# An RWKV scan with transposes shared by two chunks and two heads, and a Fourier stage over even and odd halves

## The chip, the cores and the metric

One core of one Trainium2 chip runs the whole program: a two-layer diffusion block, then a second block with an RWKV-7 mixer, an HGRN2 mixer and a mixture of experts, all in float32. The metric is the device time of one execution in microseconds. TensorE is PE in the profile (PEld its weight loads), VectorE is DVE, ScalarE is ACT, GpSimd is POOL and SyncE is SP.

## The reference, cut to what matters

Two pieces of it are touched. The Fourier mixing is a real part of a 2-D transform over tokens and the 128 channels of a group; there are four groups, once for 512 latent tokens and once for 256 context tokens:

```python
def fourier_mix(u):
    B_, L, _ = u.shape
    ug = u.reshape(B_, L, FOURIER_GROUPS, FOURIER_GROUP_DIM).astype(jnp.float32)
    f = jnp.fft.fft2(ug, axes=(1, 3), norm='ortho').real
    return f.reshape(B_, L, FOURIER_WIDTH).astype(u.dtype)
```

The RWKV scan is a recurrence over 768 tokens in either direction, for 8 heads of 64 channels:

```python
def _rwkv7_scan(r, w, k, v, a, b, s0, reverse, emit):
    def step(s, inp):
        r_t, w_t, k_t, v_t, a_t, b_t = inp
        sa = jnp.einsum('bhvk,bhk->bhv', s, a_t)
        s = s * w_t[:, :, None, :] + sa[..., None] * b_t[:, :, None, :] + v_t[..., None] * k_t[:, :, None, :]
        y = jnp.einsum('bhvk,bhk->bhv', s, r_t) if emit else None
        return s, y
```

## The kernel before, in words

The program is a row of stages, each a block with one hand-written instruction list per engine, semaphores between them and a barrier at the end. All data lies in one SBUF tensor (`arena`) and one PSUM tensor of 8 banks of 512 columns (`psum`).

**The even input stage** (`even_in`) makes, among others, u, the input of the Fourier mixing, as four tiles of 128 channels by 768 tokens. ACT copies each from PSUM. DVE has nothing to do with u; in that part of its list it copies the turned values vt.

**The Fourier stage** (`fourier`, profile lines L1421 to L1460). `channels(g)` multiplies six token tiles of group g by a 128x256 table of cosines and sines (L1421), ACT copies the result (L1453), and `tokens(g)` multiplies by token tables: for the latent tokens 4 tiles, cosine (L1431) and sine (L1432), 512 columns each, into one bank, for the context tokens 2 tiles and 256 columns (L1434, L1435). DVE copies the 768 columns of both banks (L1460), and the next group's `tokens` waits for that copy, as it writes the same banks. SP loads the tables at the end of `even_in`.

**The RWKV scan** (`rwkv_scan`). The recurrence is cut into 12 chunks of 64 tokens in each direction, 24 items, which alternate between the directions. The 8 heads stand as 4 pairs: partitions 0 to 63 hold one head of a pair (`h` = 0), 64 to 127 the other. Every product is thus 8 matmuls of 64x64, two at a time on different quarters of the array. `side_by_side(a, b)` interleaves two such products, a on the two straight quarters and b on the two crossed ones (results for the other half of the partitions). A helper makes each product's matmuls, so that the profile shows the helper's line: `same` L2301, `turned` L2304, `adding` L2316, `wide_keys` L2321, `wide_rp` L2325. One copy helper stands for all of ACT's copies (L2491).

The items pass through a pipeline of rounds r. In round r TensorE works on item r (A: the inverse of a triangular matrix by squarings), on item r-1 (B: keys, scores, and data turned for later) and on item r-2 (K: state and output), with some scores of item r+1 (L) ahead of time. The order of the products is written out by hand: sq|wz, sq|rb, w|sk, q4|pq, u1|xh, r1|xh, t|bk, pq, y3|bk, q8|y, r2|y, u2|g, v, y, r3|y (left of the bar the straight product, right the crossed one). Four of the crossed or single ones only turn data by a product with the identity, each 8 matmuls: R16 beside u1 (into bank 5, for XH), b beside t and keys beside y3 (bank 6, copied to `bkT`), values alone (bank 3, copied to `vT`). ACT copies the results of the chain out of PSUM in a fixed order: RP, Q2, Wb, Q4, U, P4, XH, Q8, U, vT, bkT. DVE masks and adds. PE waits for a copy before it writes a bank again.

**The stage after it** (`rwkv_out`) loads one table (rw_g) on SP's queue, then the first weights of the HGRN stage.

Of the kernel before, what the change touches and what calls it, by code (L numbers as in the profile page):

```python
# [1225 lines left out]
def fourier_tables(m):  # L1226
    at, W = m["at"], OFF["W"]
    return {"cos_lat": at(W, 4, LAT), "sin_lat": at(W + 4 * LAT, 4, LAT), "cos_ctx": at(W + 8 * LAT, 2, CTX),
            "sin_ctx": at(W + 8 * LAT + 2 * CTX, 2, CTX)}


def even_in(nc, m, io, feed, norm, early, mods):
# [24 lines left out]
    with st, nc.Block() as block:  # L1257
        @block.sync
        def _(sp):
# [4 lines left out]
            for name, dst in fourier_tables(m).items():  # L1264
                n = dst.shape[1] * dst.shape[2]
                lo = {"cos_lat": 0, "sin_lat": 4 * LAT, "cos_ctx": 8 * LAT, "sin_ctx": 8 * LAT + 2 * CTX}[name]
# [90 lines left out]
        def _(dve):  # L1357
# [48 lines left out]
def fourier(nc, m, early):  # L1406
# [7 lines left out]
    with st, nc.Block() as block:  # L1414
        @block.tensor
        def _(pe):
# [8 lines left out]
            def tokens(g):  # L1425
# [4 lines left out]
                for k in range(4):  # L1430
                    pe.matmul(ps[:, 6, :], x[:, k, 0:P], t["cos_lat"][:, k, :], start=(k == 0), stop=False)  # L1431
                    pe.matmul(ps[:, 6, :], x[:, k, P:2 * P], t["sin_lat"][:, k, :], start=False, stop=(k == 3))  # L1432
                for k in range(2):
                    pe.matmul(ps[:, 7, 0:CTX], x[:, 4 + k, 0:P], t["cos_ctx"][:, k, :], start=(k == 0), stop=False)  # L1434
                    mm = pe.matmul(ps[:, 7, 0:CTX], x[:, 4 + k, P:2 * P], t["sin_ctx"][:, k, :], start=False, stop=(k == 1))  # L1435
# [519 lines left out]
RW_SCRATCH = [(RW_R, 8 * T), (RW_WD, 2 * T), (RW_T1, T), (RW_Y + 4 * LAT, 4 * T - 4 * LAT)]  # L1955
# [240 lines left out]
def load_rwkv_gates(sp, m, io, sems):  # L2196
# [9 lines left out]
           "y zt yc z init wz y3 p4c")  # L2206
# [13 lines left out]
def rwkv_scan(nc, m, io, early):  # L2220
# [22 lines left out]

    RP = at(buf(2 * W4), 4, 2, C)
# [4 lines left out]
    bkT = [two_by_four() for _ in range(2)]  # L2249
    vT = [four() for _ in range(2)]  # L2250
# [41 lines left out]

    with st, nc.Block() as block:
        @block.tensor
        def _(pe):
# [32 lines left out]
            def values(j):  # L2328
                c = item(j)[1]
                v = at(RW_V, 4, T)[:, :, c * C:(c + 1) * C]  # L2330
                return lambda p, h: v[H[h], p, :]

            pe.wait_ge(s["init"], 2)
            for r in range(-1, N + 2):
# [7 lines left out]
                if A:  # L2342
                    after("pm", r + 1)
                    after("vc", r - 1)
# [8 lines left out]
                if emit_b:  # L2353
                    after("R4", r - 1)
                sq, rb = side_by_side(same(3, P16, Q16) if A else None,
# [6 lines left out]
                if K:  # L2362
                    after("ak", r - 1)
                    after("vc", r - 1)
# [4 lines left out]
                w, sk = side_by_side(adding(5, of(AR[back][:, :, 0, :]), of(vT[back]), 0, 0, False, True) if K else None,  # L2369
# [6 lines left out]
                if A:  # L2376
                    after("q2", r + 1)
                    after("bc", r - 1)
# [14 lines left out]
                u1, xh = side_by_side(same(7, of(R32), of(Wb)) if K else None, turned(5, of(R16), unit) if B else None)  # L2393
                if K:
                    u1.then_inc(s["u1"], 1)
# [15 lines left out]
                if B:  # L2411
                    after("q4c", min(r + 1, N))
                t, bk = side_by_side(same(7, of(EE[(r - 2) % 3][:, 0, :, :]), of(U), 1) if K else None,
                                     turned(6, hats(RW_B_HAT, r - 1), unit) if B else None)
                if K:
                    t.then_inc(s["t"], 1)
# [5 lines left out]
                if K:  # L2422
# [3 lines left out]
                y3, bk = side_by_side(adding(1, of(z[d]), hats(RW_R_HAT, r - 2), 1, 0, True, False) if emit_k else None,  # L2426
                                      turned(6, hats(RW_K_HAT, r - 1), unit, 1) if B else None)
                if emit_k:
                    y3.then_inc(s["y3"], 1)
                if B:  # L2430
                    bk.then_inc(s["bk"], 1)
# [1481 lines left out]
```

## Time and profile before

| | us |
|---|---|
| three runs: median (lowest to highest) | 3565.67 (3558.61 to 3571.9) |
| the profiled execution, its own time | 3560.56 |
| its span, first to last instruction | 3558.7 |
| PE busy with matmuls (share of the span) | 3244.3 (91%) |
| DVE, ACT, POOL busy | 1460.6 (41%), 922.5 (26%), 776.5 (22%) |
| mean granted PE clock | 0.972 |

The shares are means over some twenty stages with different limits. The Fourier stage lies at 262 to 311 us, the RWKV scan at 2057 to 2376 us. A profile row of PE counts passes: a float32 matmul appears as two weight loads and two matmuls, a transpose as one of each. An idle time that ends with "issue" is one in which the engine waited for nothing that the profile shows.

### The profile page before, as it was taken

The page shows a single profiled execution, that of the slowest core. Times are in us where ns is not written, and L with a number is a line of the kernel's source. Part 1 is how long each engine was busy: PE and PEld are TensorE (multiplying, and loading weights), DVE is VectorE, ACT ScalarE, POOL GpSimd, SP SyncE. Part 2 cuts the span into 40 slices and gives each one's busy share as a digit, 9 for nine tenths or more (in the row PEclk, how much of TensorE's full clock was granted, in tenths as well). Part 3 has the DMA queues.
Part 4 walks back from the last instruction along what each step waited for, and adds up shares of the span by engine and source line. Part 5 has one row for each costly group of instructions (what it writes and reads, how often), then busy time and mean ns, then how long its engine had stood idle before and what let it go on. Part 6 is the DMA issues. An engine that isn't in the chain of part 4 may idle for free. (4 is left out here: it accounts for less than half of the span.)

```text
span 3558.7 us, 67826 instructions
## 1 busy us (share of the span) xinstructions
PE 3244.3 (91%) x27492; PEld 2136.3 (60%) x27492; DVE 1460.6 (41%) x2991; ACT 922.5 (26%) x1786; POOL 776.5 (22%) x726
## 2 busy tenths in 40 slices
PE   7999999999999999999999667678988899999986
PEld 3557555555555587778865356654775465665543
DVE  1113444344332454344348744434455333333324
ACT  2112232222002253222021433334422122222211
POOL 0000332222520004333520000003311233333320
PEclk9999999999999999999999689999999999999998
DMA  5330134311211103542311000001112699999996
GB/s 227 126 113 26 36 118 170 149 60 68 65 44 63 36 1 119 213 177 94 106 45 54 0 3 5 4 18 48 60 39 77 256 366 344 361 362 354 352 398 251
DMA packets 88742, 481.04 MB, mean 135 GB/s; under 512 B 16722, under 2 KB 20850, under 8 KB 43328
## 3 DMA queue, kind: packets, MB, share of 16 engines
q1 hardware_dynamic: 72128, 439.99, 33.5%
q0 software_dynamic: 16384, 37.72, 3.2%
q8 instruction: 176, 2.88, 0.3%
q14 instruction: 54, 0.44, 0.0%
HBM read 464.80 MB, written 29.36 MB: 139 GB/s over the span
## 5 line engine op out<-in xcount | busy, mean ns | idle before, releaser
L1010 PE MATMUL psum<-arena 128*128 128x384 f32 (+1 forms) x2464 | 674.7, 434 | 5.8 <-ACT arena L599 4.8
L1010 PEld LDWEIGHTS psum<-arena 128*128 128x128 f32 x2464 | 463.5, 189 | 221.3 <-issue 22.8
L841 PE MATMUL psum<-arena 128*128 128x256 f32 (+1 forms) x1904 | 508.8, 429 | 23.4 <-PEq L3103 9.2
L841 PEld LDWEIGHTS psum<-arena 128*128 128x128 f32 x1904 | 361.5, 190 | 171.2 <-issue 26.0
L3622 PE MATMUL psum<-arena 128*64 128x256 f32 x3072 | 352.4, 378 | 15.8 <-DMA arena<-exp_w_in 15.1
L3622 PEld LDWEIGHTS psum<-arena 128*64 128x64 f32 x3072 | 231.7, 134 | 161.3 <-issue 53.6
L452 POOL TENSOR_TENSOR arena<-arena 128x512 f32<-128x512 f32 x66 | 88.2, 1336 | 1052.0 <-POOLq L1642 364.1
L1138 DVE SCALAR_TENSOR_TENSOR arena<-arena 128x511 f32<-128x511 f32 (+1 forms) x264 | 176.9, 712 | 138.1 <-ACT arena L1116 135.0
L1088 ACT ACTIVATE arena<-psum 128x384 f32<-128x384 f32 (+1 forms) x176 | 76.5, 436 | 510.3 <-PE psum L1010 510.0
L461 POOL TENSOR_TENSOR arena<-arena 128x512 f32<-128x512 f32 (+1 forms) x74 | 114.7, 1551 | 395.1 <-PE psum L1010 245.6
L3636 PE MATMUL psum<-arena 128*64 128x512 f32 x768 | 185.3, 601 | 0.2 <-DMA arena<-exp_w_in 0.2
L1132 DVE TENSOR_TENSOR arena<-psum,arena 128x384 f32<-128x384 f32 (+1 forms) x132 | 64.6, 489 | 283.4 <-PE psum L1010 283.3
L2301 PE MATMUL psum<-arena 64*64 64x64 f32 x3456 | 139.6, 223 | 36.1 <-issue 28.5
L2304 PE MATMUL psum<-arena 64*64 64x64 f32 x3328 | 129.2, 224 | 45.7 <-issue 27.1
L2807 PE MATMUL psum<-arena 128*128 128x384 f32 (+1 forms) x560 | 161.7, 450 | 4.0 <-ACT arena L599 4.0
L2491 ACT ACTIVATE arena<-psum 128x256 f32<-128x256 f32 (+1 forms) x264 | 103.6, 422 | 216.7 <-PE psum L2301 153.3
L3744 DVE SCALAR_TENSOR_TENSOR arena<-arena,psum 128x128 f32<-128x128 f32 (+1 forms) x97 | 33.8, 348 | 281.4 <-ACT arena L3695 281.4
L2301 PEld LDWEIGHTS psum<-arena 64*64 64x64 f32 x3456 | 120.8, 135 | 42.9 <-issue 33.9
L2304 PEld LDWEIGHTS psum<-arena 64*64 64x64 f32 x3328 | 115.0, 136 | 51.8 <-issue 32.5
L562 POOL TENSOR_TENSOR arena<-arena 128x1536 f32<-128x1536 f32 (+1 forms) x3 | 11.3, 3761 | 607.3 <-ACT arena L599 607.3
L2807 PEld LDWEIGHTS psum<-arena 128*128 128x128 f32 x560 | 106.9, 192 | 59.5 <-ACT arena L599 7.4
L1307 PE MATMUL psum<-arena 128*128 128x512 f32 x272 | 140.7, 598 | 0.4 <-ACT arena L599 0.4
(485 smaller groups left out, 4901.7 us busy)
## 6 DMA issues: line engine op xcount, KB each, us to landing
arena<-exp_w_in SPq DMA_DIRECT2D x207, 1024.0 KB, 10.7
arena<-w_mod_r_in SPq DMA_DIRECT2D x72, 1024.0 KB, 6.9
arena<-w_ffn_up_in SPq DMA_DIRECT2D x44, 1024.0 KB, 4.8
arena<-w_ffn_down_in SPq DMA_DIRECT2D x32, 704.0 KB, 4.1
arena<-yrows SPq DMA_DIRECT2D x8, 2048.0 KB, 23.5
arena<-w_hgrn_in SPq DMA_DIRECT2D x10, 1024.0 KB, 4.9
arena<-w_even_in_in SPq DMA_DIRECT2D x17, 512.0 KB, 3.6
arena<-w_in_in SPq DMA_DIRECT2D x15, 512.0 KB, 3.6
```

Of the source, the lines that this page charges most:

```text
L452: pool.tensor_tensor(s1, a21, a22, ADD).then_inc(s["ws"], 1)
L461: pool.tensor_tensor(a12, a12, self.piece(m, p, 5), SUB).then_inc(s["ws"], 1)
L841: mm = pe.matmul(pair_bank(ps, q, x, h), lhsT[:, k, :], rhs[:, k, :], start=(k == 0 and x in (1, 2, 7)), stop=(k == KH - 1), skip_group_ch ...
L1010: return pe.matmul(pair_bank(ps, q, x, h), feed.weights(m, q, x)[:, k, :], b.moving(x)[:, k, :], start=(k == 0 and x in (1, 2, 7)), stop=( ...
L1138: last = dve.scalar_tensor_tensor(y, x[:, lo + a:hi + e], column(q, v, tap), y, MUL, ADD)
L1307: pe.matmul(ps[:, 2 * b, :], lhsT, m["A"][:, x, 0:LAT], start=(x == 0), stop=(x == KD - 1))
L2301: return lambda p, h: pe.matmul(out(b, h, p, half), lhsT(p, h), rhs(p, h), start=True, stop=True)
L2304: return lambda p, h: pe.matmul(out(b, 1 - h, p, half), lhsT(p, h), rhs(p, h), start=True, stop=True)
L2491: return act.activation(dst, src, ACT.Copy)
L2807: mm = pe.matmul(pair_bank(ps, i, x, h), lhsT[:, k, :], rhs[:, k, :], start=(k == 0 and x in (1, 2, 7)), stop=(k == 3), skip_group_check=x ...
L3622: mm = pe.matmul(ps[64 * c:64 * c + 64, 0, 0:256], xt[u][:, k, :], wgu[w][:, k, :, c * P:(c + 1) * P], start=(k == 0), stop=(k == KD - 1))
L3636: mm = pe.matmul(ps[64 * c:64 * c + 64, 4, :], hT[:, j * 64:(j + 1) * 64], wdn[w][:, j, c * 512:(c + 1) * 512], start=(j == 0), stop=(j == 1))
```

## The change

In the Fourier stage DVE replaces each half of u's tokens by sum and difference (first half plus second, first minus second) in `even_in`. The even rows of the transform need the sums alone, the odd rows the differences: `tokens` makes 8 matmuls of 256 columns where it made 8 of 512, and 4 of 128 where it made 4 of 256. The tables have half the rows; DVE's copy becomes two, which put even and odd rows back in order.

In the scan b, keys and values of two neighbouring chunks of a direction are turned together, in the round of the first of them (`leads`, 12 of 24 items, always two such rounds after each other): four transposes of 128x128 each, into banks 6, 3 and 2. ACT takes each apart with four copies of 64 partitions, into one of four buffers `bkv`, three times per lead round. R16 is turned by two 128x128 transposes in every round, and the copy XH becomes five. The scratch for it takes the place of the mask rst64, which is loaded again after the scan.

```diff
 def fourier_tables(m):
-    return {"cos_lat": at(W, 4, LAT), "sin_lat": at(W + 4 * LAT, 4, LAT), "cos_ctx": at(W + 8 * LAT, 2, CTX),
-            "sin_ctx": at(W + 8 * LAT + 2 * CTX, 2, CTX)}
+    return {"cos_lat": at(W, 2, LAT), "sin_lat": at(W + 2 * LAT, 2, LAT), "cos_ctx": at(W + 4 * LAT, 1, CTX),
+            "sin_ctx": at(W + 4 * LAT + CTX, 1, CTX)}
...
+                if kind == "u":
+                    u = at(EV_U + i * T, T)
+                    dve.wait_ge(s["act"], tiles["u", i] + 1)
+                    for lo, mid, hi in ((0, LAT // 2, LAT), (LAT, LAT + CTX // 2, T)):
+                        own.link(dve.tensor_tensor(u[:, mid:hi], u[:, lo:mid], u[:, mid:hi], SUB))
+                        dve.scalar_tensor_tensor(u[:, lo:mid], u[:, lo:mid], 2.0, u[:, mid:hi], MUL, SUB)
...
+                for name, bank, first, tiles, half in (("lat", 6, 0, 2, LAT // 2), ("ctx", 7, 4, 1, CTX // 2)):
+                    for odd in range(2):
+                        part = slice(odd * half, (odd + 1) * half)
+                        for k in range(tiles):
+                            for j, table in enumerate(("cos_", "sin_")):
+                                mm = pe.matmul(ps[:, bank, part], x[:, first + odd * tiles + k, j * P:(j + 1) * P],
+                                               t[table + name][:, k, part], start=(k == 0 and j == 0),
+                                               stop=(k == tiles - 1 and j == 1))
...
-                dve.tensor_copy(A[:, g, :], pair_banks(ps, 3, T)).then_inc(s["oc"], 1)
+                for bank, lo, hi in ((6, 0, LAT), (7, LAT, T)):
+                    o = dve.tensor_copy(A[:, g, lo:hi].rearrange("p (j a) -> p a j", a=2),
+                                        ps[:, bank, 0:hi - lo].rearrange("p (a j) -> p a j", a=2))
+                o.then_inc(s["oc"], 1)
...
+    TURNED = (6, 3, 2)
+    bkv = [at(buf(3 * W4), 3, 4, C) for _ in range(4)]
...
+    def leads(j):
+        return active(j) and j // 2 % 2 == 0
+    def pairs(j):
+        return 2 * (j // 4) + j % 2 + 1
...
+            def by_tokens(j, t):
+                d, c, _ = item(j)
+                src = at((RW_B_HAT[d], RW_K_HAT[d], RW_V)[t], 4, T)
+                c -= c % 2
+                for p in range(4):
+                    mm = pe.transpose(ps[:, TURNED[t], 2 * p * C:2 * (p + 1) * C], src[:, p, c * C:(c + 2) * C], ident)
+                return mm
+            def inverse_turned():
+                for q in range(2):
+                    mm = pe.transpose(ps[:, 5, 2 * q * C:2 * (q + 1) * C], flat(R16)[:, 2 * q * C:2 * (q + 1) * C], ident)
...
                 if A:
                     after("pm", r + 1)
-                    after("vc", r - 1)
+                    if r >= 2:
+                        after("kc", pairs(r - 2))
...
-                u1, xh = side_by_side(same(7, of(R32), of(Wb)) if K else None, turned(5, of(R16), unit) if B else None)
+                    side_by_side(same(7, of(R32), of(Wb)), None)[0].then_inc(s["u1"], 1)
+                if B:
+                    inverse_turned()
...
-                t, bk = side_by_side(same(7, of(EE[(r - 2) % 3][:, 0, :, :]), of(U), 1) if K else None,
-                                     turned(6, hats(RW_B_HAT, r - 1), unit) if B else None)
+                    side_by_side(same(7, of(EE[(r - 2) % 3][:, 0, :, :]), of(U), 1), None)[0].then_inc(s["t"], 1)
+                if leads(r - 1):
+                    by_tokens(r - 1, 0).then_inc(s["bt"], 1)
+                    after("rbm", r - 8)
+                    after("R4", r - 1)
+                    by_tokens(r - 1, 2).then_inc(s["v"], 1)
...
-                y3, bk = side_by_side(adding(1, of(z[d]), hats(RW_R_HAT, r - 2), 1, 0, True, False) if emit_k else None,
-                                      turned(6, hats(RW_K_HAT, r - 1), unit, 1) if B else None)
+                    side_by_side(adding(1, of(z[d]), hats(RW_R_HAT, r - 2), 1, 0, True, False), None)[0].then_inc(s["y3"], 1)
...
                 if B:
                     after("xc", r)
                     after("rbm", r - 8)
+                    after("vc", pairs(r - 1))
...
-                if B:
+                if leads(r - 1):
                     after("q8c", min(r + 1, N))
-                    v = side_by_side(None, turned(3, values(r - 1), unit))[1]
-                    v.then_inc(s["v"], 1)
+                    by_tokens(r - 1, 1).then_inc(s["kt"], 1)
...
+            def tokens(j, t):
+                for half in range(2):
+                    to = bkv[(j if item(j)[1] % 2 == half else j + 2) % 4]
+                    for h in range(2):
+                        done = copy(to[H[1 - h], t, :, :], twos(TURNED[t])[H[half], :, h, :])
+                return done
...
-                    copy(flat(XH), bank(5)).then_inc(s["xc"], 1)
+                    copy(XH[:, 1, :, :], bank(5, 1))
+                    x = bank(5, 0).rearrange("p (q h) c -> p q h c", q=2)
+                    for p in range(2):
+                        for h in range(2):
+                            turned = copy(XH[H[1 - h], 0, p::2, :], x[H[p], :, h, :])
+                    turned.then_inc(s["xc"], 1)
+                if leads(r - 1):
+                    after("v", pairs(r - 1))
+                    after("y", r - 2)
+                    tokens(r - 1, 2).then_inc(s["vc"], 1)
...
-                if active(r - 1):
-                    j = r - 1
-                    after("v", r)
-                    after("y", j - 1)
-                    copy(vT[j % 2], bank(3, 0)).then_inc(s["vc"], 1)
-                    after("bk", r)
-                    copy(flat(bkT[j % 2]), bank(6)).then_inc(s["bc"], 1)
+                if leads(r - 1):
+                    after("bt", pairs(r - 1))
+                    tokens(r - 1, 0).then_inc(s["bc"], 1)
+                    after("kt", pairs(r - 1))
+                    tokens(r - 1, 1).then_inc(s["kc"], 1)
...
             sp.dma_start(g2, io["rw_g2_2"]).then_inc(s["w"], 16)
+            sp.dma_start(m["rst64"], io["rst64"]).then_inc(s["rst"], 16)
             then.load(m, sp, 0)
+            sp.wait_ge(s["rst"], 16)
```

How the instructions stand in a lead round, in three places. On PE before, from the last matmuls of r1|xh over t beside the turning of b (L2301 and L2304 in turn) and pq (the rest of the L2304 x10) to the start of y3 (L2316):

```order
L2304 MATMUL psum<-arena 64x64 x2
L2301 MATMUL psum<-arena 64x64 x2
L2304 MATMUL psum<-arena 64x64 x2
L2301 MATMUL psum<-arena 64x64 x2
L2304 MATMUL psum<-arena 64x64 x2
L2301 MATMUL psum<-arena 64x64 x2
L2304 MATMUL psum<-arena 64x64 x2
L2301 MATMUL psum<-arena 64x64 x2
L2304 MATMUL psum<-arena 64x64 x10
L2316 MATMUL psum<-arena 64x64 x2
```

And now, with lines moved by some 19 (t L2320, transposes of b and values L2353, pq L2323, y3 L2335):

```order
L2323 MATMUL psum<-arena 64x64 x2
L2320 MATMUL psum<-arena 64x64 x8
L2353 MATMUL psum<-arena 128x128 x8
L2323 MATMUL psum<-arena 64x64 x8
L2335 MATMUL psum<-arena 64x64 x8
```

The crossed product beside t is gone and t and y3 stand alone; eight transposes over the whole array stand between t and pq in lead rounds only.

On PE, the piece from u2|g to the round's last group; before, the values are 8 of the L2304 x10:

```order
L2301 MATMUL psum<-arena 64x64 x2
L2304 MATMUL psum<-arena 64x64 x10
L2316 MATMUL psum<-arena 64x64 x8
L2301 MATMUL psum<-arena 64x64 x2
L2316 MATMUL psum<-arena 64x64 x2
```

Now, with the keys' transposes (L2353) in that place:

```order
L2320 MATMUL psum<-arena 64x64 x2
L2323 MATMUL psum<-arena 64x64 x2
L2353 MATMUL psum<-arena 128x128 x4
L2335 MATMUL psum<-arena 64x64 x8
L2320 MATMUL psum<-arena 64x64 x2
```

The values moved up past five groups, the keys moved down past three.

On ACT, one whole round before: RP, then Q2 to P4, XH, then Q8, U and vT, bkT:

```order
L2491 ACTIVATE arena<-psum 128x4x64
L2491 ACTIVATE arena<-psum 128x256 x5
L2491 ACTIVATE arena<-psum 128x512
L2491 ACTIVATE arena<-psum 128x256 x3
L2491 ACTIVATE arena<-psum 128x512
```

Now a lead round: RP, then Q2 to P4 and XH's second half, four quarters of XH's first half, the values, Q8 and U, and b and keys:

```order
L2524 ACTIVATE arena<-psum 128x4x64
L2524 ACTIVATE arena<-psum 128x256 x6
L2524 ACTIVATE arena<-psum 64x2x64 x4
L2524 ACTIVATE arena<-psum 64x256 x4
L2524 ACTIVATE arena<-psum 128x256 x2
L2524 ACTIVATE arena<-psum 64x256 x8
```

The copies of turned data, XH's included, became 17 where three stood, and eight of them are the last that ACT does before the next round's RP.

## Rows read from the trace of the kernel before

**Rows 1.** Windows: stretch, length, busy us (count) per engine, clock, DMA

```profile
2080.00:2350.00 270.00, 188.50 (x8681) 173.04 (x8682) 115.56 (x260) 91.94 (x235) 0.00 (x0) 1.00 0.02 4
268.80:311.30 42.50, 40.27 (x123) 22.62 (x121) 3.83 (x4) 4.35 (x3) 0.00 (x0) 1.00 0.00 0
355.00:372.00 17.00, 10.72 (x41) 6.47 (x37) 9.61 (x19) 9.89 (x34) 2.74 (x1) 0.61 0.01 1
```

**Rows 2.** Waits of PEld, 2080.2 to 2350.2: us, times, longest

```profile
PEld psum L2304 <- issue: 32.5, 24, 2.1
PEld psum L2301 <- issue: 31.6, 39, 2.0
PEld psum L2316 <- issue: 17.5, 18, 2.0
...
PEld psum L2301 <- ACT arena L2491: 2.6, 10, 0.4
```

**Rows 3.** DMA view, 2080 to 2350: TensorE's instruction queue; packets, MB, share

```profile
q8 instruction: 69, 1.13, 1.8%
```

**Rows 4.** Windows, as rows 1: two RWKV stretches, one HGRN stretch

```profile
2197.10:2200.90 3.80, 2.62 (x125) 2.41 (x126) 1.85 (x5) 1.04 (x3) 0.00 (x0) 1.00 0.02 4
2200.90:2204.80 3.90, 2.58 (x126) 2.44 (x125) 1.44 (x3) 1.64 (x4) 0.00 (x0) 1.00 0.02 4
...
2591.40:2595.10 3.70, 3.70 (x134) 3.70 (x131) 2.12 (x5) 1.62 (x3) 0.00 (x0) 1.00 0.02 4
```

**Rows 5.** Timeline of PEld, two restarts: start, us, what, [idle before <-releaser]

```profile
2200.92 0.19 PEld L2321 LDWEIGHTS psum<-arena 64*64 64x64 f32 x2 [1.10 <-issue]
...
2204.82 0.13 PEld L2301 LDWEIGHTS psum<-arena 64*64 64x64 f32 x1 [1.47 <-issue]
```

**Rows 6.** Timeline, TensorE, the kernel's last stage: transposes in a row

```profile
3494.32 1.92 PE L3646 MATMUL psum<-arena 128*128 128x128 f32 x16
```

**Rows 7.** Timeline of PE, experts: 64-wide tiles, the whole array, 64-wide tiles

```profile
3003.84 0.71 PE L3509 MATMUL psum<-arena 64*128 64x64 f32 x8
3004.67 0.33 PE L3628 MATMUL psum<-arena 128*128 128x128 f32 x1
3004.93 0.64 PE L3503 MATMUL psum<-arena 128*64 128x5 f32 x16
```

**Rows 8.** Timeline, scan's end: u1, the copy U, and t

```profile
2368.16 0.54 PEld L2301 LDWEIGHTS psum<-arena 64*64 64x64 f32 x16 [0.61 <-ACT arena L2491]
...
2368.89 0.38 ACT L2491 ACTIVATE arena<-psum 128x256 f32<-128x256 f32 x1 [0.78 <-PE psum L2301]
...
2369.32 0.54 PEld L2301 LDWEIGHTS psum<-arena 64*64 64x64 f32 x16 [0.62 <-ACT arena L2491]
```

**Rows 9.** Lines by form, scan, ACT: us busy, mean ns | idle before

```profile
L2491 ACT ACTIVATE arena<-psum 128x256 f32<-128x256 f32 x215 | 79.7, 384 | 213.7 <-PE psum L2301 150.5 <-DVE arena L2567 35.2 <-PE psum L2316 16.8
...
L2491 ACT ACTIVATE arena<-psum 128x512 f32<-128x512 f32 x48 | 28.4, 592 | 0.1
```

**Rows 10.** Timeline, ACT in the scan: two copies back to back

```profile
2198.82 0.66 ACT L2491 ACTIVATE arena<-psum 128x256 f32<-128x256 f32 x2 [2.53 <-PE psum L2301]
```

**Rows 11.** Timeline, Fourier token stage of the last group

```profile
301.38 1.10 PE L1431 MATMUL psum<-arena 128*128 128x512 f32 x2 [1.14 <-DVE arena L1460]
...
308.32 0.60 PE L1434 MATMUL psum<-arena 128*128 128x256 f32 x2
...
310.25 0.96 DVE L1460 COPY arena<-psum 128x768 f32<-128x768 f32 x1 [9.02 <-PE psum L1435]
```

**Rows 12.** Timeline, DVE in the even input stage: the first two copies of vt

```profile
185.44 0.96 DVE L1390 COPY arena<-psum 128x768 f32<-128x768 f32 x1 [4.75 <-PE psum L1297]
198.45 0.96 DVE L1390 COPY arena<-psum 128x768 f32<-128x768 f32 x1 [12.05 <-PE psum L1297]
```

**Rows 13.** Timeline, the stage after the scan: rw_g's issue and who waits

```profile
2375.93 0.33 SPq L2634 DMA_DIRECT2D arena<-rw_g_in  x1
...
2378.63 0.29 PEld L2647 LDWEIGHTS psum<-arena 128*128 128x128 f32 x1 [0.60 <-DMA arena<-rw_g_in]
```

More of the change, by code:

```diff
@@ L1954 @@
 RW_Y = RW_KK
-RW_SCRATCH = [(RW_R, 8 * T), (RW_WD, 2 * T), (RW_T1, T), (RW_Y + 4 * LAT, 4 * T - 4 * LAT)]
+RW_SCRATCH = [(RW_R, 8 * T), (RW_WD, 2 * T), (RW_T1, T), (OFF["rst64"], T), (RW_Y + 4 * LAT, 4 * T - 4 * LAT)]
 RW_JOBS = [("c", 4), ("c", 5), ("c", 6), ("s", 0), ("c", 7), ("s", 1), ("c", 0), ("s", 2), ("c", 1), ("s", 3), ("c", 2), ("c", 3),
@@ L2248, in rwkv_scan @@
     XH = two_by_four()
-    bkT = [two_by_four() for _ in range(2)]
-    vT = [four() for _ in range(2)]
     RB = [four() for _ in range(2)]
@@ L2326, in wide_rp @@
                                               start=True, stop=True)
[L2328 to L2331, printed above, removed]
+            def by_tokens(j, t):
[8 more added lines that the diff above has]
+                    mm = pe.transpose(ps[:, 5, 2 * q * C:2 * (q + 1) * C], flat(R16)[:, 2 * q * C:2 * (q + 1) * C], ident)
+                return mm
             pe.wait_ge(s["init"], 2)
@@ L2354, in _ @@
                     after("R4", r - 1)
+                    if r >= 2:
+                        after("vc", pairs(r - 2))
                 sq, rb = side_by_side(same(3, P16, Q16) if A else None,
@@ L2363, in _ @@
                     after("ak", r - 1)
-                    after("vc", r - 1)
+                    after("vc", pairs(r - 2))
                     after("wz", r - 1)
@@ L2368, in _ @@
                     after("yc", r - 10)
-                w, sk = side_by_side(adding(5, of(AR[back][:, :, 0, :]), of(vT[back]), 0, 0, False, True) if K else None,
+                w, sk = side_by_side(adding(5, of(AR[back][:, :, 0, :]), of(bkv[(r - 2) % 4][:, 2, :, :]), 0, 0, False, True) if K else None,
                                      wide_keys(r - 1) if B else None)
@@ L2377, in _ @@
                     after("q2", r + 1)
-                    after("bc", r - 1)
+                    if r >= 2:
+                        after("bc", pairs(r - 2))
                 if L:
@@ L2436, in _ @@
                 if K:
-                    after("bc", r - 1)
+                    after("bc", pairs(r - 2))
+                    after("kc", pairs(r - 2))
                     after("y3", r - 9)
                 q8, y = side_by_side(same(3, of(P4), of(Q4)) if A else None,
-                                     adding(1, of(bkT[back][:, 1, :, :]), of(vT[back]), 0, 1, not emit_k, False) if K else None)
+                                     adding(1, of(bkv[(r - 2) % 4][:, 1, :, :]), of(bkv[(r - 2) % 4][:, 2, :, :]), 0, 1, not emit_k, False) if K else None)
                 if A:
@@ L2446, in _ @@
                 r2, y = side_by_side(same(4, of(Q4), r_now) if A else None,
-                                     adding(1, of(vT[back]), of(AR[back][:, :, 1, :]), 1, 1, False, False) if emit_k else None)
+                                     adding(1, of(bkv[(r - 2) % 4][:, 2, :, :]), of(AR[back][:, :, 1, :]), 1, 1, False, False) if emit_k else None)
                 if A:
@@ L2477, in _ @@
                 r3, y = side_by_side(same(4, of(Q8), r_now) if A else None,
-                                     adding(1, of(bkT[back][:, 0, :, :]), of(U), 0, 1, False, True) if K else None)
+                                     adding(1, of(bkv[(r - 2) % 4][:, 0, :, :]), of(U), 0, 1, False, True) if K else None)
                 if A:
@@ L2622, in rwkv_out @@
 def rwkv_out(nc, m, io, then):
-    st, s = stage(nc, "rwo", "w mm1 mm2 mm3 yc sq lg rt t1 yn af fin own")
+    st, s = stage(nc, "rwo", "rst w mm1 mm2 mm3 yc sq lg rt t1 yn af fin own")
     at, ps, cols = m["at"], m["ps"], m["cols"]
```

18 lines of the change are left out of this document (4 added, 14 removed).

## The prediction

> **What bounds the kernel now.** I read the stretches first. The middle of the RWKV scan (2080 to 2350 us) has TensorE matmuls busy for 188.5 of 270 us at the full clock, ACT for 92 and DVE for 116; the Fourier token stage (268.8 to 311.3) has TensorE busy for 40.3 of 42.5 us and DVE for 3.8 [rows 1]. So Fourier is bound by TensorE's columns. In the scan TensorE is idle for almost a third of the time, and the waits say for what: ACT ended 2.6 us of it, while 81.6 us (three rows, some 80 times, up to 2.1 us) are "issue", with no other engine behind it [rows 2]. The DMA view gives the cause: in these 270 us TensorE's instruction queue landed 69 packets of 16 KB, one per 3.91 us [rows 3]. Two stretches cut at the restarts show one packet each: some 126 matmul passes and 126 weight loads, issued in 2.4 us, then nothing [rows 4]; the restarts carry idle times of 1.10 and 1.47 us before them, 3.90 us apart [rows 5]. The HGRN scan, where such a stretch takes 3.70 us to issue, has no idle time at all [rows 4]. So the RWKV scan is paced by its number of TensorE instructions: 8681 passes in 69 packets, 126 passes per 3.91 us, as long as running them, waits included, takes less.
>
> The Trainium skill (Runtime: NRT & Kernel Launch, Instruction fetch mechanics) has the 256-instruction blocks of 16 KiB, but calls their boundary mostly hidden. Here the 81.6 us of [rows 2] are not; what follows if it held is a rival below.
>
> **The scan.** A matmul is two passes: the 8 of u1 in the program show as 16 loads [rows 8]; 4928 matmuls are 78 packets. Each of 24 items loses four turnings of 8 matmuls, 64 passes (R16 beside u1, b beside t, keys beside y3, values alone): 1536. A 128x128 transpose is one pass (16 rows for 2 x 8 of them [rows 6]); 2 per item and 12 per lead round (12 of the 24 rounds with an item to turn) make 192. 1344 passes fewer are 10.7 packets; some 50 more wait instructions take 0.4 back. **10.3 x 3.91 = 40 us** go if packets still pace it all.
>
> Does the run still fit under 3.91 us per packet? Before, an item is 3.26 packets, so 3.26 x 2.41 = 7.9 us of issue. A two-sided group of 32 passes costs 32/126 x 2.41 = 0.61 us; a one-sided group of 16, 0.54 less its last load, 0.41 [rows 8]. Three groups shrink (-0.6) and the values go (-0.4). Transposes come 0.11 us apart [rows 6]: +0.22 per item, +1.31 in a lead round. A change between 64-wide tiles and the whole array has one row: after a lone 128x128 transpose the next matmul starts 0.26 us later instead of 0.11 [rows 7], so 0.15; before it at most 0.12 more lie idle. I take 0.15 for each of 2 changes per round, 6 in a lead round. Run: lead 7.9 - 1.0 + 0.22 + 1.31 + 0.9 = 9.3 us, other rounds 7.9 - 1.0 + 0.22 + 0.3 = 7.4.
>
> The Trainium skill (TensorEngine Tiling (Array Packing), Key Properties) speaks against the change here: switching the tiling mode, not just the tile, drains TensorE. The 0.15 us of [rows 7] agree; were changes free, the runs would be 8.4 and 7.1 us and the scan, below, about 4 us better.
>
> Then the waits. ACT's copies replace TensorE's work: of 256 columns 384 ns, of 512 592 [rows 9], back to back 0.28 us apart [rows 10]; by the slope 128 columns take about 0.18. Per round XH goes from one copy (0.49) to five (0.28 + 4 x 0.18 = 1.0), and a lead round adds 12 copies of half the partitions, three times 1.12 us, for two rounds' 0.28 + 0.49. In a lead round, from the end of r1|xh2: DVE's R1 to 0.65, P4 to 1.0, XH to 2.0, values to 3.15, Q8 to 3.4 (a hop to ACT is 0.19, the copy 0.38 and back 0.05 [rows 8]). TensorE meanwhile does t, b and values (1.43), pq2, y3, q8, r2 (3.3), u2|g (3.8), keys (4.4), yu, r3 (5.5), and waits for nothing. But the copy U waits for u2, ends at 4.4, and the copies of b and keys stand behind it: keys ready at 6.65. The next round's first group needs their bank (kc), so TensorE waits **1.2 us**. Behind it on the queue stands the whole round; ACT's RP and Q2 wait with it.
>
> Lead round: 9.3 + 1.2 = 10.5 us against 411 - 64 + 14 = 361 passes, 2.87 packets, 11.2 us; other rounds 7.4 against 349 passes, 10.8. On average all is covered, but the 1.2 us and the keys fall into one packet, whose run is then about 4.2, and packets are not in step with rounds. I take 0.8 us lost per lead round, 10 us; bounds 0 and 2.5 us (the wait, six changes and what the fetch then adds, uncovered), 30 us. **Scan: -30 us, bounds -40 and -10.**
>
> **Fourier.** The last group's token stage runs from 301.38 over 308.32 to the copy at 310.25 [rows 11]: 16 passes of 512 columns, 0.43 us apart, then 8 of 256, half as far apart, 8.6 us. Now 16 of 256 and 8 of 128 (0.11, [rows 6]): 4.3. Four groups: -17.1. Two copies instead of one of 0.96 [rows 11] cost perhaps 0.15 each time, twice on the path (before the fourth group, at the end): +0.3, bounds 0 and 2. **-16.8.** Half the table bytes: worth nothing, as TensorE is at channels while they land. The folding of u, 16 DVE instructions of about 0.3 us, lies in DVE's idle time before the four copies of vt (4.75 us before the first, 12.05 before the second [rows 12]); if that cover failed, vt would come 1.2 us late per tile, 5 us in all.
>
> **After the scan.** rst64 (0.39 MB) follows rw_g on SP's queue, ahead of w_hgrn. TensorE waited 0.6 us for rw_g, 2.7 us after its issue [rows 13]. Shared engines could make that later: 0 to 4 us, nearest the row's own wait: +0.5. The end of SP's block waits for rst64, which has the whole stage to land.
>
> **Sum.** -30 - 16.8 + 0.5 = -46.3 us. The profiled execution took 3560.6 us and gives 3514.3; the median of the three runs, 3565.7, stands 5.1 higher and gives 3519.4. I forecast the middle, **3517 us**, and price the rivals from the same middle, 3563.1.
>
> **Rivals.**
> - *All waits covered* (0.13): the scan keeps -40, -57 in all: 3506. For it: 3.5 us to spare in every second round. Against: the wait for kc sits in one packet.
> - *The copies pace the lead rounds* (0.15): ACT's tail grows where a packet comes late before u2, and both delays add: scan -10, 3537. For it: ACT has 6.6 us of copies in a lead round (six of 0.28, XH 1.0, twelve of 0.28, Q8 and U), 2.2 of them behind u2.
> - *The boundary is no cost of its own* (0.04): the idle time hides something else, and the run counts. Then lead rounds gain 1.4 us and others lose 0.5: scan +11, 3558. Against: one packet per idle time, 69 times. The Trainium skill's page named above (Runtime: NRT & Kernel Launch) leads here.
> - *The clock falls in the scan* (0.05), the one that ends slower. Waits for kc beside waits for packets leave TensorE idle for longer at a time; in the GLA stretch of [rows 1], where it waits for ACT and DVE, the granted clock was 0.61, half speed (1.2 of 2.4 GHz) for most of it. At half the clock a packet's 2.9 us of run are 5.8, 1.9 over the pace; 25 of the 68 packets use up the 46 us, and 34 make it 3582. Against: through idle times up to 2.1 us the clock stood.
> - The change not doing what it says (transposes in two passes, say, +6 us) or something unseen: 0.03.
>
> **How the numbers follow.** The forecast has 0.60, by itself 3503 to 3530. The range 3501 to 3538 adds the covered case and the copies; left out are the last two rivals and some of the tails. About 0.5% (18 us) is what a measurement of this kernel can tell from no change. Faster by more: forecast, covered and most of the copies, 0.88. Within it: a bad case of the copies, the boundary: 0.07. Slower: the clock, 0.05.
>
> **What would show it.** About 68 instruction packets in the scan instead of 78, still about 3.9 us apart; the scan some 30 us shorter; a new wait of TensorE for ACT of about 1.2 us after lead rounds, in all 5 to 15 us; transposes 0.11 apart; the token stage 25.5 us; clock 1.00 throughout the scan. Wrong it is if packets come faster or slower than 3.9 us with the new mix, if TensorE's waits for ACT exceed 30 us, or if the clock row in the scan falls.

## The result, and the profile after

The changed kernel takes 3540.8 us (median of 6 runs, 3533.5 to 3545.5) beside 3565.6 us of the kernel before (6 runs): ratio 0.9932, 95% interval 0.9923 to 0.9942, so 24.8 us faster. The forecast was 3517 us, some 46 us faster, range 3501 to 3538. The profiled execution took 3537.2 us (span 3535.4).

Windows of the changed kernel, columns as in [rows 1]: the Fourier token stage, the scan's middle, and 3 us of the scan:

```profile
268.80:294.40 25.60, 22.92 (x121) 20.20 (x119) 4.09 (x8) 4.35 (x3) 0.00 (x0) 1.00 0.00 1
2080.00:2330.00 250.00, 202.04 (x7332) 181.00 (x7336) 111.05 (x251) 135.34 (x392) 0.00 (x0) 0.95 0.02 4
2081.00:2084.00 3.00, 3.00 (x101) 2.92 (x97) 0.42 (x1) 1.04 (x3) 0.00 (x0) 0.50 0.03 5
```

The token stage does the work of 42.5 us of [rows 1] in some 25.6. The scan's middle now runs 7332 passes in 250 us, 29.3 per us; before it was 8681 in 270, 32.2 per us. So passes are fewer, and they come more slowly. ACT is busy for 54% of the time in place of 34%, and the clock is no longer 1.00: seven stretches of 3.4 us, the third line lies in one, ran at 0.50, half speed.

The DMA view, 2080 to 2330 us, TensorE's instruction queue as in [rows 3]:

```profile
q8 instruction: 59, 0.97, 1.6%
```

That is one packet per 4.24 us, where [rows 3] had one per 3.91. The traces show where a packet holds TensorE up, if its instructions (matmuls, loads and waits) are counted in blocks of 256. In the scan's middle before, a pause of at least 0.6 us stands at the start of every block, 69 times of 69, and ends 1.4 us after a packet has landed. In the changed kernel only 17 of 58 blocks begin with a pause of over 0.4 us: packets no longer pace most of it. The waits of PEld in the same stretch (us, times, longest):

```profile
PEld psum L2320 <- issue: 44.1, 48, 2.5
PEld psum L2323 <- issue: 7.7, 18, 1.1
PEld psum L2335 <- ACT arena L2524: 4.6, 13, 0.6
```

The first line reads as if nothing but issue were waited for, as in [rows 2]. It needs the timeline to see that this is no longer true. ACT behind u2 of round 18 (they run from -1 to 25; the copies are U, then four of b, four of the keys), and PEld:

```profile
2269.39 3.53 ACT L2524 ACTIVATE arena<-psum 128x256 f32<-128x256 f32 x9 [0.46 <-PE psum L2320]
```

```profile
2270.64 0.26 PEld L2335 LDWEIGHTS psum<-arena 64*64 64x64 f32 x6
2272.99 0.17 PEld L2320 LDWEIGHTS psum<-arena 64*64 64x64 f32 x2 [2.10 <-issue]
```

The nine copies end at 2272.92; TensorE's next group, the one that waits for kc, starts at 2272.99. The same 0.07 us lies between the two in every round of this kind: the "issue" of 2.10 us is the wait for the keys' copy. There are 12 such waits, of 1.7 to 2.55 us. The nine copies also give their spacing: (3.53 - 0.38) / 8 = 0.39 us. ACT's copies by form (us busy, mean ns of one):

```profile
L2524 ACT ACTIVATE arena<-psum 128x256 f32<-128x256 f32 x216 | 77.5, 383 | 149.5 <-PE psum L2320 96.8 <-DVE arena L2615 37.2 <-PE psum L2335 12.9
L2524 ACT ACTIVATE arena<-psum 64x256 f32<-64x256 f32 x144 | 54.4, 378 | 2.1
L2524 ACT ACTIVATE arena<-psum 64x128 f32<-64x128 f32 x96 | 26.2, 272 | 1.1
```

A copy of 64 partitions lasts as long as one of 128 (378 and 383 ns), but two of 128 start 0.28 us apart [rows 10], two of 64 start 0.39.

From stage start to stage start, the Fourier stage fell from 49.9 to 32.8 us (-17.1) and the scan from 316.0 to 306.7 (-9.3). The stage behind the scan is unchanged (33.0, 32.9). The two profiled executions lie 23.3 us apart; the experts (+2.6) and the GLA scan (+1.6) were longer in the second, and the cause of that is open.

### The profile page after: what moved, and what is told of

Its sections match the earlier page's. It is cut to its first block and busy times, and to the rows that moved or that the text cites. A ratio compares the mean times of both kernels' runs of the same rounds, so it can differ in the third digit from the quotient of the medians.

```text
span 3535.4 us, 65390 instructions
## 1 busy us (share of the span) xinstructions
PE 3248.2 (92%) x26148; PEld 2151.9 (61%) x26148; DVE 1464.6 (41%) x3011; ACT 976.3 (28%) x1978; POOL 776.0 (22%) x726
## 5 line engine op out<-in xcount | busy, mean ns | idle before, releaser
L2524 ACT ACTIVATE arena<-psum 128x256 f32<-128x256 f32 (+2 forms) x456 | 158.1, 358 | 152.8 <-PE psum L2320 96.8
L2320 PE MATMUL psum<-arena 64*64 64x64 f32 x3456 | 145.1, 230 | 47.2 <-issue 30.0
L2320 PEld LDWEIGHTS psum<-arena 64*64 64x64 f32 x3456 | 126.6, 142 | 59.8 <-issue 48.7
L1307 PE MATMUL psum<-arena 128*128 128x512 f32 x272 | 140.8, 598 | 1.3 <-ACT arena L599 1.3
L3600 POOL TENSOR_TENSOR arena<-arena 128x1 f32<-128x1 f32 x195 | 38.9, 199 | 397.1 <-DVE arena L3789 391.6
L2021 PE MATMUL psum<-arena 128*128 128x512 f32 x240 | 116.7, 592 | 0.8 <-ACT arena L599 0.8
```

The lines of the kernel that those rows point to most:

```text
L1307: pe.matmul(ps[:, 2 * b, :], lhsT, m["A"][:, x, 0:LAT], start=(x == 0), stop=(x == KD - 1))
L2021: mm = pe.matmul(ps[:, 2 * b, :], lhsT, m["A"][:, k, 0:LAT], start=(k == 0), stop=(k == KD - 1))
L2320: return lambda p, h: pe.matmul(out(b, h, p, half), lhsT(p, h), rhs(p, h), start=True, stop=True)
L2524: return act.activation(dst, src, ACT.Copy)
```

## The experiments

All runs in one table. Ratios are to the kernel before, timed on the same chip. From the profile of each: the scan from TensorE's first to last instruction; the sum of 12 lead rounds and of the 12 others (from one round's first TensorE instruction to the next's); the mean period of 256 TensorE instructions, one packet, in the scan's middle. The scan of `fourier_only` is that of the kernel before, so the scan column scatters by some 3 us, the two sums by 2 to 2.5 and the period by 0.06.

| run | ratio (95%) | scan | lead | other | period |
|---|---|---|---|---|---|
| before | 1 | 313.2 | 147.4 | 146.9 | 3.91 |
| after | 0.9932 (0.9923-0.9942) | 303.9 | 164.5 | 120.3 | 4.32 |
| fourier_only | 0.9949 (0.9933-0.9966) | 310.2 | 144.9 | 144.8 | 3.85 |
| dve_b | 0.9891 (0.9874-0.9907) | 291.5 | 149.0 | 122.0 | 4.08 |
| dve_b_bank6 | 0.9939 (0.9923-0.9956) | 304.8 | 155.2 | 129.2 | 4.32 |
| two_copies | 0.9948 (0.9932-0.9965) | 279.9 | 135.5 | 125.2 | 3.94 |
| old_xh | 0.9934 (0.9917-0.9951) | 310.9 | 162.7 | 127.8 | 4.25 |
| dve_b_old_xh | 0.9878 (0.9862-0.9895) | 292.0 | 147.8 | 123.7 | 3.96 |
| fill_wait | 0.9930 (0.9914-0.9947) | 307.6 | 165.9 | 122.2 | 4.31 |
| split_v | 1.0023 (1.0012-1.0034) | 325.1 | 151.3 | 154.7 | 3.90 |
| spread | 0.9867 (0.9847-0.9887) | 289.9 | 141.4 | 128.1 | 4.05 |
| spread_old_xh | 0.9900 (0.9881-0.9918) | 295.4 | 145.1 | 131.1 | 4.05 |
| dve_b_half_k | 0.9887 (0.9870-0.9903) | 290.8 | 143.0 | 126.9 | 4.08 |

The rows "before" and "after" say where the gain went: the 12 rounds without turnings gained 26.6 us, the lead rounds gave 17.1 back. The two are not independent: the others now take 10.0 us for the 2.67 packets they hold, 3.75 us each, under the 3.89 of both kinds before. That packets land while the lead round ahead of them waits would explain it; no run shows that by itself. The theory (A in most expectations): the lead rounds are paced by ACT's queue of 64-partition copies, the others by packets. Its rivals: packets pace both; the clock; the two parts of the change disturb each other.

**Fourier alone.** The edit: only the diff's parts in `fourier_tables`, `even_in`, `fourier` and `shape_constants`.

> The kernel before with the Fourier part of the change alone (half tables, folded u, the mixing's matmuls by even and odd halves, two copies per group); the scan stays as before. Theory A (the Fourier term was right, the shortfall lies in the scan): 3565.6 - 17 = 3548 to 3549, so that the scan part of the change is worth only 8 of the 24.8 us. Theory B (the two parts disturb each other, each alone would give what was forecast): clearly away from -17, and the scan's part away from -8.

Measured 3542.0 beside 3559.4: -17.4 us (by the ratio 12 to 24). The scan's part was not run alone; what is left for it, some 7 us, agrees with the -9.3 of its stage in the profile. The missing gain is the scan's.

**b's copies on VectorE.**

```diff
 # ACT
-                    after("bt", pairs(r - 1))
-                    tokens(r - 1, 0).then_inc(s["bc"], 1)
 # DVE, behind R2
+                if leads(r - 1):
+                    after("bt", pairs(r - 1))
+                    after("y", r - 2)
+                    tokens(r - 1, 0).then_inc(s["bc"], 1)
```

(Left out here: VectorE's own `tokens`, the same loop with its copy.)

> The changed kernel with the four copies of b's tokens moved from ScalarE to VectorE, which makes them early (behind its second doubling sum); keys and values stay on ScalarE. Nothing is left out. Theory A (lead rounds are paced by ScalarE's queue of 64-partition copies, 0.39 us apart: TensorE waits 2.1 to 2.6 us for the keys' copy at the head of the round behind): keys are copied 1.57 us earlier, the wait falls to about 0.6 us in 12 rounds, -18 us, and with the long waits the stretches at half clock go (up to -8 us more): 3515 to 3523. Theory B (instruction packets pace the lead rounds too, the wait only takes the place of theirs): within 4 us of the changed kernel's 3541, the idle time moving to the packets' ends.

Measured 3521.2 beside 3559.4 of the kernel before: 0.0041 in ratio under the changed kernel, about 15 us, and the intervals lie apart. A had asked for 18 to 26 under the changed kernel, B for at most 4. The same place in round 18, ACT and PEld:

```profile
2261.31 1.55 ACT L2524 ACTIVATE arena<-psum 64x256 f32<-64x256 f32 x4 [0.27 <-PE psum L2353]
```

```profile
2261.96 0.26 PEld L2335 LDWEIGHTS psum<-arena 64*64 64x64 f32 x6
2262.93 0.17 PEld L2320 LDWEIGHTS psum<-arena 64*64 64x64 f32 x2 [0.71 <-issue]
```

Only the keys' four stand behind u2 now, they end at 2262.86, and "issue" shrinks from 2.10 to 0.71 us: a copy decided it, and the keys' last copy still ends 0.07 us ahead of the group in all 12 rounds (waits of 0.7 to 1.2 us). The clock over the scan's middle is 1.00.

**Two copies of 128 partitions.**

```diff
-                for half in range(2):
-                    to = bkv[(j if item(j)[1] % 2 == half else j + 2) % 4]
-                    for h in range(2):
-                        done = copy(to[H[1 - h], t, :, :], twos(TURNED[t])[H[half], :, h, :])
+                for h in range(2):
+                    done = act.activation(bkv[(j + 2 * h) % 4][:, t, :, :], twos(TURNED[t])[:, :, h, :], ACT.Copy, scale=0.0)
```

> The changed kernel with two copies of 128 partitions x 256 for each token set in place of four of 64 x 256, scaled by zero, so that b, keys and values are zero in the scan: it leaves out the regrouping by chunk and head and the scan's contents, not the order of the work. Theory A (a copy of 64 partitions does not start before the one ahead has ended, one of 128 does): the copies start 0.28 us apart, a set takes 0.66 us in place of 1.57, three sets save 2.7 us in each of 12 lead rounds; the wait for the keys' copy falls from 2.2 us to under 0.6, about -20 us. Theory B (copies out of a transposed bank or into these buffers are slow by themselves): two copies 0.39 us apart, a set 0.8 us, and a smaller gain of about -15 us.

The scan fell to 279.9 us, 24.0 under the changed kernel's; the lead rounds to 135.5. The whole time did not, since zeros in the scan route the tokens differently: from the first expert instruction to the last it is 804.4 us in place of 779.7. The scan is the number to read. U, then b's and the keys' copies (timeline), and the scan's middle (windows):

```profile
2250.24 0.38 ACT L2524 ACTIVATE arena<-psum 128x256 f32<-128x256 f32 x1 [0.83 <-PE psum L2320]
2250.52 1.21 ACT L2529 ACTIVATE arena<-psum 128x256 f32<-128x256 f32 x4
```

```profile
2080.00:2305.00 225.00, 193.15 (x7174) 171.18 (x7177) 110.99 (x250) 104.89 (x325) 0.00 (x0) 1.00 0.02 4
```

(1.21 - 0.39) / 3 = 0.27 us apart, as [rows 10], for the same columns out of the same banks. With them the packets' period is 3.94 us, and 7174 passes in 225 us are 31.9 per us, the pace of [rows 1]. So with short copies the scan is 33 us under the kernel before's, where the forecast had 30. But a set takes some 0.6 us here and not the 1.12 of the forecast, and of the 0.9 us saved per set (1.57 to 0.66) 0.8 would come from there being two copies and not four, at 0.39 us each (an estimate). The run shows that copy time held the lead rounds up, not what the overlap of neighbours alone is worth.

**More packets.** The kernel before, the values turned in halves:

```diff
-                    v = side_by_side(None, turned(3, values(r - 1), unit))[1]
+                    for part in range(2):
+                        n = slice(part * 32, (part + 1) * 32)
+                        for p in range(4):
+                            for h in range(2):
+                                v = pe.matmul(out(3, 1 - h, p)[:, n], values(r - 1)(p, h), unit(p, h)[:, n], start=True, stop=True)
```

> The kernel before with each of the eight 64x64 matmuls that turn the values issued as two of 32 columns: 8 passes, 16 instructions more per item, the same columns in total. Nothing is left out. Theory A (the scan before is paced by the packets of instructions at 3.91 us each): 24 x 16 = 384 instructions are 1.5 packets, +5.9 us: scan 313 to 319, time 3559 to 3565 beside the kernel before's run of that time, in the same call +5 to +7. Theory B (the pause at the packets' ends is cover for the waits of the round, and running time counts): the added passes run 0.03 us each, inside it, +0 to +1 us; the packets' period then falls below 3.91 us.

Measured +8.2 us (ratio 1.0023, so 4.3 to 12.1); B's 0 to 1 is outside. A's price was counted too low: eight matmuls more are 16 passes and 16 loads, 32 instructions per item. The trace has 10240 passes in the scan where the kernel before has 9856, so 768 instructions or 3.0 packets more, and A should have said +11.7 us, still inside the interval. The profiled scan grew by 11.9. The queue still lands

```profile
q8 instruction: 69, 1.13, 1.8%
```

in 2080 to 2350 us, exactly as [rows 3], while the scan grew. Three packets more cost three packets' time, within the scatter.

**Filling the wait.**

```diff
+                if leads(r - 2):
+                    for _ in range(2):
+                        pe.matmul(bank(7), ident, at(RW_MASKS, 8 * C), start=True, stop=True)
```

> The changed kernel with two 128x512 matmuls of constants into bank 7 (free there, result not used) ahead of the wait for the keys' copy, in the 12 rounds that have it: TensorE works through most of the wait. Nothing is left out. Theory A (the half-clock stretches follow from TensorE's standing idle in these waits, and each costs about 1.2 us of the scan): seven stretches of 3.4 us at 0.5 vanish, the scan's middle shows a clock of 1.00, -4 to -8 us: 3533 to 3537. Theory B (the clock falls for another reason, or costs nothing because packets are waited for anyway): clock stays at 0.94 to 0.95, or the time stays within 3 us of 3541.

Half of A came true. Windows:

```profile
2080.00:2330.00 250.00, 212.74 (x7309) 177.43 (x7310) 110.39 (x250) 134.35 (x388) 0.00 (x0) 1.00 0.02 4
2081.00:2084.00 3.00, 2.38 (x115) 2.11 (x116) 0.43 (x1) 1.32 (x4) 0.00 (x0) 1.00 0.02 5
```

With TensorE busy in the wait the clock stays at 1.00; seven falls became none, where two profiles of one scan (`before`, `fourier_only`) have none and two. So the falls went with its idle time there. But the ratio is 0.9930 beside 0.9932, and in 10 of 12 rounds the wait ends as before, 0.1 us behind the keys' last copy: the falls cost nothing that these runs resolve. In the 3 us that ran at 0.50 the window counts 101 matmul passes, at 1.00 it is 115. The very passes of the seven stretches took 23.0 us there and 18.3 in `fill_wait`, 0.7 us a stretch more (from 0.2 less to 1.4 more); the whole time shows nothing of it.

**The inverse's turning undone** (eight matmuls beside u1 and one copy `copy(flat(XH), bank(5))` again).

> The changed kernel with one part undone: the inverse is turned as before by eight 64x64 matmuls beside u1, and XH is one copy of 128x512 in place of five. Nothing is left out. Theory A (in lead rounds ScalarE's queue of copies is the bound, in the others the packets): XH costs 0.6 us in place of 1.5, so the keys' copy comes 0.9 us earlier in 12 rounds, -11 us and fewer stretches at half clock; 6 more passes per item are 1.1 packets, +4.5 us: 3531 to 3537 against the changed kernel's 3541. Theory B (every part that saves passes pays): the change's two transposes per item are worth their packets, so undoing them costs +4 us: 3545.

Measured 0.9934: no gain. The price of the instructions was again counted too low, in this and the next expectation and in that of `spread_old_xh`: the trace has 8848 passes where the changed kernel has 8512, 14 more per item and not 6, so 2.6 packets, +10.3 us and not 4.5. With that A comes to about -1 us, and +0.7 was measured by ratio; B comes to +10, outside the interval. A's mechanism came true in part only: in 10 of 12 rounds the wait for the keys is still 1.7 to 2.55 us, the lead rounds are 1.8 us shorter in sum and the others 7.5 longer. The wait's length is set behind u2, by U, b and the keys on ACT (3.53 us above), against 1.5 us of TensorE's work; XH lies ahead of u2 and shifts both.

> Both repairs: b's token copies on VectorE, and the inverse turned as before with one copy of XH. Nothing is left out. With b on VectorE TensorE still waited 0.8 to 1.3 us for the keys in 12 rounds. Theory A (copies there, packets elsewhere): that falls by up to 0.9 us each, -8 us, and 1.1 packets more are +4.5 us: 3514 to 3520 against 3521. Theory B (once b is gone from ScalarE's queue, packets pace the lead rounds too): +4 us, 3525.

Measured 0.9878 beside 0.9891 for `dve_b`: inside each other's intervals, not settled (with 2.6 packets A is +2 us, B +10).

**b on VectorE, keys into bank 6** (`TURNED = (6, 6, 2)`; the keys' transposes wait for bc, q4 for kc, sq for neither).

> As the run with b on VectorE, and the keys are turned into bank 6 behind b in place of bank 3, so that the next round's first step no longer waits for the keys' copy (the fourth step does). Nothing is left out. Theory A (copies paced it, packets are next): no wait for keys is left, 59 packets at 3.9 us, the scan's middle 250 us falls to about 232, and the half-clock stretches vanish: 3505 to 3515, near the forecast of 3517 that the packets' count gave. Theory B (packets are no bound once fewer, something else, such as the longer chain from v's copies to the Gram step, holds the lead rounds): no better than the run with b on VectorE.

Measured 0.9939, worse than `dve_b`: A missed, and B's "no better" holds, though by a wait that it had not named. The waits of PEld:

```profile
PEld psum L2353 <- DVE arena L2593: 12.8, 10, 1.8
```

The keys' transposes now wait on TensorE's own queue for VectorE's copies of b, and the last two groups of the round stand behind them. A wait was traded for one further up the queue.

**Spreading the copies.** Values on VectorE behind w2, half of the keys there behind R4, b on ACT ahead of Q8:

```diff
 # DVE, behind w2, and behind R4
+                    tokens(r - 1, 2).then_inc(s["vc"], 1)
+                    tokens(r - 1, 1, (0,)).then_inc(s["kc"], 1)
 # ACT, ahead of Q8, and last
+                    tokens(r - 1, 0).then_inc(s["bc"], 1)
+                    tokens(r - 1, 1, (1,)).then_inc(s["kc"], 1)
```

> The changed kernel with its 64-partition token copies spread over two engines: VectorE makes the four of the values (between its add to Wb and the doubling's masking) and two of the four of the keys (behind its add to R32), ScalarE the four of b ahead of Q8 and the other two of the keys. Nothing is left out. Theory A (copies pace the lead rounds, packets the rest): no wait for the keys is left that is longer than 0.3 us, lead rounds come to about 136 to 140 us in sum (164.5 in the changed kernel, 135.5 in the run with two copies per set), the scan to about 282, ratio to the kernel before 0.985 to 0.987, some 3513 to 3517. Theory B (VectorE now holds up the next round's mask, inverse or Gram step): no better than the run with b alone on VectorE, 0.989.

> The same spread, and the inverse turned as before with one copy of XH. Nothing is left out. Theory A (with the copies off the path, packets pace every round): 6 passes more per item are 1.1 packets, +4.5 us against the spread run, some 0.987 to 0.988 of the kernel before. Theory B (XH's five copies still stand ahead of the keys' and the values'): -3 to -8 us against the spread run.

`spread` took 3519.2 beside 3563.4: 0.9867, where A has 0.985 to 0.987 and B 0.989; its interval (0.9847 to 0.9887) lies under the changed kernel's. TensorE's idle time ahead of the round behind a lead round is at most 0.5 us. But the scan is 289.9, not 282: the other rounds grew to 128.1, from 122.0 in `dve_b`. `spread_old_xh` at 0.9900 is on A's side (slower), with overlapping intervals; by its 2.6 packets A is +10.3 us, the profiled scan grew by 5.5. A last arrangement, b on VectorE behind w2 and half the keys there:

> The changed kernel with the four copies of b on VectorE right behind its add to Wb, two of the four of the keys on VectorE behind its add to R32, the values and the other two of the keys on ScalarE. Nothing is left out. In the spread run the values waited for VectorE, and the Gram step for them; here each engine begins its set as soon as it is turned. Theory A (ScalarE's queue paced the lead rounds, and what the spread run lacked to the two-copies run is lateness on VectorE): lead rounds some 138 us in sum, scan 283 to 288, ratio to the kernel before 0.984 to 0.987. Theory B (VectorE's four copies ahead of the doubling's mask cost as much as those of the values): as the spread run, 0.987.

Measured 0.9887, no better than `spread` (B). Apart from `dve_b_bank6`, all five arrangements that take copies off ACT's tail beat both kernels by ratio, with intervals under the changed kernel's; among them the runs hardly choose. What keeps the scan at 290 and not 280 wasn't isolated; VectorE's own copies, 0.43 us apart each in its list of masks and adds, are the likely cause, not a shown one.

## Where the prediction held, and where it failed

- **Fourier, -16.8:** measured -17.1 in the profile and -17.4 by itself. The halving of the columns and the copies were right: the two copies of a group take 1.02 us, one took 0.96 [rows 11]. Folding u cost nothing that shows (the even input stage takes 210.9 us before and after), and rst64, priced at +0.5, neither.
- **Packets, 10.3 x 3.91 = -40:** the count and the price per packet hold. The scan has 68.0 blocks of 256 instructions in place of 78.3, and the price is 3.91 us before, 3.94 where the copies are short and there are 1344 passes fewer, 3.90 with 768 instructions more. From its first to its last instruction's start a packet took 2.56 us on average before and 3.38 in `two_copies`, and the pause behind it went from 1.35 to 0.54: the period stood, so the run is covered by the fetch, as argued, though in `two_copies` 25 of 57 blocks already begin without a pause of 0.4 us. The Trainium skill (Runtime: NRT & Kernel Launch, Instruction fetch mechanics) calls the boundary mostly hidden; in the scan before no block's boundary was, and `split_v` speaks against it, while in the changed kernel, whose blocks run longer, 41 of 58 were.
- **The waits, 10 us lost (0.8 per lead round, bounds 0 and 2.5): the step that failed.** The mechanism was named in its place: U, b and keys behind u2, the next round's first group waiting for kc. Its size was off, first of all by one number. "Back to back 0.28 us apart [rows 10]" was read from copies of 128 partitions and used for copies of 64, of which the trace before had none on ACT, without a bound for that. A set takes 1.57 us, not 1.12; XH 1.5, not 1.0. From the end of r1|xh2 U is through after 5.1 us, not 4.4 (the values' copies are late for g, and Q8 with them), and the keys after 8.3, not 6.65. TensorE waits 2.2 us on average, not 1.2, and in round 18 0.38 for the values and 0.27 ahead of Q8, that were at nothing. The keys' 1.65 us are 20 us in 12 lead rounds (an estimate from these rows), about what the scan's -9.3 falls short of -30.
- **TensorE's run, 9.3 us in a lead round:** too small as well. Idle times under 0.08 us counted in, it is at work for 10.4 us of a lead round where the sum had 9.3, and for 8.8 of a round before where it had 7.9; so the base was low, and the growth of 1.6 (forecast 1.4) about right. The changes of tile width are in that growth: a 64-wide matmul starts 0.20 us after the transpose ahead of it, where transposes start 0.11 apart. With the waits and 0.5 us of pauses for packets, lead rounds took 13.7 us, where the 2.77 packets that they hold would take 10.8 at 3.91 us and the forecast had 0.8 more on top of its packets; the others took 10.0 (10.4 for 2.67 packets). That `two_copies` gains more than these terms is no check of them, as its sets are shorter than the forecast's.
- **Rivals.** That the copies pace the lead rounds (scan -10, 3537) is what happened: scan -9.3. I had argued it from packets that come late before u2; it needs none. That the clock falls came true as an event and failed as a price: it fell in seven stretches, and filling the waits to keep it up gained nothing. It is one of the prediction's own signs of being wrong, and so are packets slower than 3.9 us (4.32 on average): neither was the cause, both went with the waits.

## What to carry to other kernels

Where a stage is paced by its count of instructions, saving them pays only until the work that replaces them on another engine is longer than the packets saved; price that work round by round, from the last event it needs to the first that needs it. A copy's row holds for its own number of partitions: half the partitions was no cheaper here, and lost the overlap of neighbours. Count a change's instructions as the trace counts them, passes and loads: four expectations here had half of it or less. And an idle time labelled "issue" is to be held against the end of the copy its code waits for before it is put down to fetching.

## What was not expected of the hardware

- Neighbouring ACT copies of 128 partitions overlap by 0.1 us (start 0.28 apart, last 0.38); with a copy of 64 partitions on either side the next starts 12 to 25 ns after the end of the one ahead. Copies that move to the other half of the partitions and those that stay were alike.
- In the changed kernel's scan the granted clock fell to 0.50 for 3.4 us seven times, each time after TensorE (neither a matmul nor a load running) had been idle for 1.9 to 2.4 us. The length of one idle time does not decide it alone: four more of 1.9 to 1.96 us in the same trace were followed by no fall, nor were those of up to 1.95 us before, while in `fourier_only`, with the scan of before, it fell twice, behind 1.63 and 1.69 us. What else decides it is open.
- Half the clock did not double the time: the passes of these seven stretches took 23.0 us, and 18.3 in `fill_wait` at 1.00.
- Wherever TensorE pauses for a packet, in any of these runs, it starts again 1.4 us after the landing (1.36 to 1.40 on average in each). The next packet's fetch starts 1.4 us after that restart (1.3 to 1.6) and takes 1.1 us. The three make the 3.9 us, whether the block itself ran for 2.56 us or 3.38.
